# One transformer layer in fp32: 40 projection panels as quarter products, both branch projections behind them

## The reference, cut to what matters

```python
h = rmsnorm(x, norm_mix_g)                      # x: 512 tokens x 2048, float32
q_a, k_a, v_a, q_b, k_b, v_b = split(h @ w_in)  # widths 1024, 256, 256, 1024, 1024, 1024
o_a = swa_sink_attention(rope(q_a), rope(k_a), v_a, sinks)
o_b = stick_breaking_attention(q_b, k_b, v_b)
y_a, y_b = o_a @ w_branch_a, o_b @ w_branch_b   # 1024 -> 2048
gates = sigmoid(h @ w_gate + b_gate).reshape(S, 2, 2048)
x = x + (gates[:, 0] * y_a + gates[:, 1] * y_b) @ w_out
x = x + memory_cross_attention(rmsnorm(x), rmsnorm(mem), ...)
x = x + swiglu(rmsnorm(x), w_gu, w_down)        # hidden width 5632
return rmsnorm(x)
```

## Time and profile before

| | |
|---|---|
| median of three runs | 2746.04 us |
| the profiled execution: span, first to last instruction (what lies around it has no record of its own) | 2743.1 us |
| TensorE busy | 2704.5 us |
| VectorE busy | 1737.1 us |
| ScalarE busy | 1017.7 us |
| GpSimd busy | 766.3 us |
| HBM read and written | 301.27 and 30.41 MB |

### The profile page before, as it was taken

One profiled execution on the slowest core, in us unless ns is written; L12 is line 12 of the kernel. 1 busy time (PEld: TensorE's weight loads), 2 busy tenths in 40 slices (PEclk: granted clock), 3 DMA queues, 4 the chain that ended last, 5 costly groups with the idle time before them and its releaser, 6 DMA issues.

```text
span 2743.1 us, 34950 instructions
## 1 busy us (share of the span) xinstructions
PE 2704.5 (99%) x13710; PEld 2279.2 (83%) x13710; DVE 1737.1 (63%) x1820; ACT 1017.7 (37%) x1134; POOL 766.3 (28%) x642
## 2 busy tenths in 40 slices
PE   9999999999999999999999999999999999999997
PEld 7888888888778888888788888888888888888886
DVE  6677652334653344573677767687777777777786
ACT  6555432224642232243553333333333332222224
POOL 0000000000000003330357666776667632212120
PEclk9999999999999999999999999999999999999999
DMA  6221233322222325333434444434343463444432
GB/s 239 77 85 62 83 97 99 92 84 92 77 93 92 99 77 207 93 121 109 139 109 137 132 138 132 138 101 146 127 143 127 143 238 123 161 146 137 161 125 82
DMA packets 125889, 333.29 MB, mean 121 GB/s; under 512 B 10320, under 2 KB 57424, under 8 KB 125136
## 3 DMA queue, kind: packets, MB, share of 16 engines
q1 hardware_dynamic: 119296, 309.37, 35.3%
q10 hardware_dynamic: 6480, 22.35, 2.0%
HBM read 301.27 MB, written 30.41 MB: 121 GB/s over the span
## 4 chain that ended last, share of the span: by engine, by line
PE 92%; DVE 4%; ACT 1%; DMA 1%; issue 1%; SPq 0%; DVEq 0%; ACTq 0%
PE ps L2198 16%; PE acc L1812 14%; PE acc L1814 14%; PE acc L1813 14%; PE ps L2201 8%; PE acc L1832 6%; PE acc L1834 6%; PE acc L1833 6%; PE acc L2198 3%; PE acc L2201 1%; DMA x_tokens<-x_n 1%; PE ps L1874 1%; PE ps L1863 1%; DVE w_lo L1588 1%; ACT ps L799 0%
## 5 line engine op out<-in xcount | busy, mean ns | idle before, releaser
L1101 DVE TENSOR_TENSOR w_lo<-raw,w_hi 128x1024 fp32r<-128x1024 f32 x328 | 475.9, 1456 | 274.9 <-ACT w_hi L609 274.3
L1812 PE MATMUL acc<-act_both,w_hi 128*128 128x512 f32 (+1 forms) x1536 | 591.1, 385 | 3.6 <-DVE w_lo L1101 3.1
L1814 PE MATMUL acc<-act_both,w_lo 128*128 128x512 f32 (+1 forms) x1536 | 585.3, 381 | 0.0
L1813 PE MATMUL acc<-act_both,w_hi 128*128 128x512 f32 (+1 forms) x1536 | 584.9, 381 | 0.0
L609 ACT ACTIVATE w_hi<-raw 128x1024 fp32r<-128x1024 f32 x328 | 344.3, 1055 | 553.9 <-PE acc L1814 340.7
L1812 PEld LDWEIGHTS acc<-act_both,w_hi 128*128 128x128 f32 x1536 | 289.6, 189 | 59.4 <-DVE w_lo L1101 3.7
L1814 PEld LDWEIGHTS acc<-act_both,w_lo 128*128 128x128 f32 x1536 | 289.5, 188 | 55.4
L1813 PEld LDWEIGHTS acc<-act_both,w_hi 128*128 128x128 f32 x1536 | 289.8, 189 | 54.3 <-issue 0.7
L543 POOL MEMSET mem_stat<- 128x256 f32 x1 | 0.3, 312 | 1047.1 <-DMA mem<-mem_t 1047.1
L2198 PE MATMUL ps<-t_both,w_hi 128*128 128x512 f32 x896 | 281.6, 396 | 0.5 <-DVE cg L1616 0.5
L1832 PE MATMUL acc<-act_both,w_hi 128*128 128x512 f32 x672 | 262.9, 391 | 3.1 <-DVE x L1456 3.0
(11 more groups left out here) (306 smaller groups left out, 4752.8 us busy)
## 6 DMA issues: line engine op xcount, KB each, us to landing
raw<-w_stream SPq DMA_DIRECT2D x412, 512.0 KB, 3.6
over<-w_stream SPq DMA_DIRECT2D x84, 512.0 KB, 4.4
gate_t<-cg ACTq DMA_DIRECT2D x22, 512.0 KB, 2.6
over<-gate_t SPq DMA_DIRECT2D x22, 512.0 KB, 5.3
up_t<-cu ACTq DMA_DIRECT2D x20, 512.0 KB, 2.6
over<-up_t SPq DMA_DIRECT2D x20, 512.0 KB, 6.2
x<-x_t SPq DMA_DIRECT2D x16, 512.0 KB, 8.6
x_tokens<-x_n SPq DMA_DIRECT2D x4, 1024.0 KB, 15.4
```

The source lines that it names most:

```text
L1101: nc.vector.tensor_tensor(w_lo[:, s, :], raw[:, s, :], f(w_hi[:, s, :]), ALU.subtract)\
L1812: nc.tensor.matmul(dst, wh, ah, start=start and k == 0, stop=False)
L1813: nc.tensor.matmul(dst, wh, al, start=False, stop=False)
L1814: last = nc.tensor.matmul(dst, wl, ah, start=False, stop=stop and k == UK - 1)
```

## The change

The order of the weight stream and of all engines' programs from 365 us on is new:

- Only v0, v1, k0 and q0 stay direct panels (8 units, `U_V`); the first four of these units are multiplied inside `sb_last`, where gate units were.
- k1, q1 to q7 and all 32 gate panels become 20 pairs of quarter products (`U_H`, 80 mix units). For this GpSimd scales `x` by the norm's gain and makes its sums during stick-breaking, ScalarE and VectorE split them (`mixed_high`, `mixed_low`), and every pair goes out to HBM (`h_t`) and comes back later.
- The stick-breaking result goes out raw (`ob_t`) instead of being split on chip; it is read back and split at the end of the quarter products (`ob_high`, `ob_low`).
- The 16 units of branch projection B (`U_BB`) are the fillers of local attention, now one unit each (`FILLERS` 3, 3, 3, 2 with 3 ahead and 2 behind). ScalarE copies each product to `merged` (`branch_copy`).
- The 16 units of branch projection A (`U_BA`) follow. For each pair of outputs VectorE scales four gate tiles by the norm (L1690, 128 x 2048), ScalarE takes four sigmoids, and VectorE multiplies and adds.

In all, 120 direct units between stick-breaking's last pass and the output projection (the four inside it included) become 40 direct units and 80 mix units.

```diff
+U_V = U_SB + PAIRS * 6
+U_H = U_V + 4 * 2
+H_PAIRS = 4 + 2 * KT // 2
+H_UNITS = 4 * H_PAIRS
+U_BB = U_H + H_UNITS
+U_BA = U_BB + KT
+U_OUT = U_BA + KT
-FILLERS = (4, 6, 3, 3)
+FILL_FIRST, FILL_LAST = 3, 2
+FILLERS = (3, 3, 3, 2)
...
             def o_high(par_):
-                nc.scalar.activation(o_hi[rows, pair.at(), :], ps[par_][rows, 0:S], ACT.Copy)\
-                    .then_inc(o_hi_done, 1)
+                nc.scalar.activation(zb[par_][rows, 0:S], ps[par_][rows, 0:S], ACT.Copy).then_inc(ps_free, 1)
+                act.wait_ge(ps_free, hd.at(3 + par_))
+                act.dma_start(ob_t[pair.at(), rows, :], zb[par_][rows, 0:S]).then_inc(ob_stored[par_], 16)
...
+            mixed_low(0, 0)
+            while converted.n < U_H:
+                units()
+            mixed_low(1, 0)
+            mix_low(5)
+            for p in range(H_LOOPS):
+                dve.wait_ge(pair_stored[1], 16 * p) if p else None
+                read_products(2 * p, cg)
+                mix_low(2)
...
+                if p < H_LOOPS - 1:
+                    mix_low(2)
+                else:
+                    mix_low()
+                    ob_low(0)
+                    units()
+                    ob_low(1)
+                dve.wait_ge(pair_stored[0], 16 * (p + 1))
+                read_products(2 * p + 1, cu)
+                if p < H_LOOPS - 1:
+                    mix_low(4)
...
             for d in range(DUOS):
                 swa_max(d, 0)
                 swa_max(d, 1)
                 swa_prob(d, 0)
+                units()
                 swa_prob(d, 1)
                 if d < DUOS - 1:
                     rope(ROTATED[d][0])
-                    units(2)
+                    units()
                     rope(ROTATED[d][1])
...
+            for j in range(KT // 2):
+                part = gates_of(j)
+                dve.wait_ge(gates_in[j % 4], 32 * (j // 4 + 1))
+                nc.vector.tensor_tensor(part, part, rstd[:].unsqueeze(1).unsqueeze(1).broadcast_to([P, 2, 2, S]),
+                                        ALU.mult).then_inc(gates_scaled, 1)
+                for b in range(2):
+                    m = 2 * j + b
+                    if converted.n < U_OUT + AHEAD:
+                        units()
+                    ga, gb, dst = part[:, 0, b, :], part[:, 1, b, :], merged[:, m, :]
+                    dve.wait_ge(acc_free, A_BB + m + 1)
+                    dve.wait_ge(sig_ready, 4 * j + 2 * b + 1)
+                    link(nc.vector.tensor_tensor(dst, dst, gb, ALU.mult))
+                    dve.wait_ge(sig_ready, 4 * j + 2 * b + 2)
+                    unit.add()
+                    dve.wait_ge(unit_done, unit.at())
+                    nc.vector.tensor_tensor(ga, output()[:], ga, ALU.mult).then_inc(acc_free, 1)
+                    dve.wait_ge(acc_free, out_no.at())
+                    nc.vector.tensor_tensor(dst, dst, ga, ALU.add).then_inc(mix_ready, 1)
+                if j > 1:
+                    merged_low(2 * j - 4, 2)
+            while converted.n < U_OUT + AHEAD:
+                units()
+            merged_low(KT - 4, 4)
...
+            for d in range(DUOS):
+
+                swa_scores(d, 0)
+                swa_scores(d, 1)
+                filler()
+                swa_turn(d, 0)
+                filler()
+                swa_values(d, 0)
+                swa_turn(d, 1)
+                filler(FILLERS[d] - 2)
+                swa_values(d, 1)
+            filler(FILL_LAST)
+            for m in range(KT):
+                unit(output()[:], [oa_tile(k) for k in range(UK)], True, True,
```

More of the change, by code:

```diff
@@ L240, in block_kernel @@
         with ExitStack() as a:
+            sb("place_of_products", [P, 22 * UK * P // 4], F32, a)
             cos_t = sb("cos_t", [P, S], F32, a)
             sin_t = sb("sin_t", [P, S], F32, a)
+        with ExitStack() as a:
+            gate_pairs = [sb(f"gate_pair{n}", [P, 2, 2, S], F32, a) for n in range(2)]
+        with ExitStack() as a:
             ka = sb("ka", [P, S], F32, a)
@@ new lines, in mix_sums @@
+            def mix_sums(first, end):
+                for n in range(first, end):
+                    part = mix_raw(n)
+                    pool.wait_ge(mix_in[n % 4], 16 * (n // 4 + 1))
+                    link(nc.gpsimd.tensor_tensor(part[:, 4, :], part[:, 0, :], part[:, 1, :], ALU.subtract))
+                    link(nc.gpsimd.tensor_tensor(part[:, 5:7, :], part[:, 0:5:4, :],
+                                                 part[:, 3:4, :].broadcast_to([P, 2, 2 * P]), ALU.add))
+                    nc.gpsimd.tensor_tensor(part[:, 7, :], part[:, 2, :], part[:, 6, :], ALU.subtract)\
+                        .then_inc(sums_made, 1)
@@ L851, in merged_high @@
                     nc.scalar.activation(act_hi[:, m, :], merged[:, m, :], ACT.Copy).then_inc(mg_hi, 1)
-            gates(gate_a, B_GATE, merged_high)
+            for j in range(KT // 2):
+                act.wait_ge(gates_scaled, j + 1)
+                for b in range(2):
+                    for a, first in ((1, KT), (0, 0)):
+                        sigmoid(gates_of(j)[:, a, b, :], B_GATE + first + 2 * j + b)
+                    units()
+                if j > 1:
+                    merged_high(2 * j - 4, 2)
+            while converted.n < U_OUT + AHEAD:
+                units()
+            act.wait_ge(unit_done, U_OUT)
+            merged_high(KT - 4, 4)
+            out_no.n = A_OUT
             with repeat(act, KT // 4, [(converted, 4)]):
@@ new lines, in _ @@
+            mixed_low(0, 0)
+            while converted.n < U_H:
+                units()
+            mixed_low(1, 0)
+            unit.n = U_BB
+            out_no.n = A_BB
+            mix_low(5)
+            for p in range(H_LOOPS):
+                dve.wait_ge(pair_stored[1], 16 * p) if p else None
+                read_products(2 * p, cg)
+                mix_low(2)
+                if p == 0:
+                    angles()
+                if p == 1:
+                    two_angles()
+                if p == 2:
+                    scaled_angles()
+                if p < H_LOOPS - 1:
[3 more added lines that the diff above has]
+                    ob_low(0)
+                    units()
+                    ob_low(1)
+                dve.wait_ge(pair_stored[0], 16 * (p + 1))
+                read_products(2 * p + 1, cu)
+                if p < H_LOOPS - 1:
+                    mix_low(4)
@@ L1417, in _ @@
                 tr.add()
-            units(2)
-            rope(1)
-            units(2)
+            units()
             rope(2)
-            units(2)
+            units()
             for d in range(DUOS):
@@ new lines, in mix_groups @@
+            def mix_groups(first, end, outputs):
+                for g in range(first, end):
+                    if g - first < 2:
+                        pe.wait_ge(acc_free, outputs - 1 + g - first)
+                    for c in range(4):
+                        if g == 0 and c in (0, 2):
+                            pe.wait_ge(t_lo_done, 4 + 2 * c)
+                        mix_unit(g, c)
+            panel(act_tile)
+            panel(act_tile)
+            assert u.n == U_H and out_no.n == A_BB
@@ L2038, in _ @@
                 tr.add()
-            for _ in range(3):
-                panel(act_tile)
+            filler()
             pe.wait_ge(va_ready, 2)
-            fill = Tally()
-            def filler():
-                if fill.n % 2 == 0:
-                    fill_dst.append(output()[:])
-                unit(fill_dst[-1], second if fill.n % 2 else first, fill.n % 2 == 0, fill.n % 2 == 1)
-                fill.add()
-            fill_dst = []
             for d in range(DUOS):
@@ L2306 @@
 HEADS = [h + o * GQ for h in LOWER for o in (0, 1)]
-def gates_and_branches(w_gate, w_branch):
-    gates, branches = ([stream(columns(w, m)) for m in range(KT)] for w in (w_gate, w_branch))
-    parts = gates[:2]
-    for m in range(0, KT, 2):
-        parts += branches[m:m + 2] + gates[m + 2:m + 4]
-    return parts
 def weight_stream(w_in, w_gate, w_a, w_b, w_out, w_xq, w_xkv, w_xo, w_gu, w_down):
```

661 lines of the change are left out of this document (362 added, 299 removed).

## The result

The change makes the kernel slower: 2855.68 us median (2854.62 to 2857.44) against 2746.24, a ratio of 1.0401 with a 95% interval of 1.0386 to 1.0415. The forecast was 2813 with a range up to 2845: the sign was right, the size too small by 43 us.

The account below looks back on a forecast made before the run. TensorE was taken to bound the kernel. Terms -43.4, +1, +1, +9, +11.5, +71.4 and +17 gave +67.5 us on the profiled 2743.1, so 2810.6; with 2.9 for the median, 2813 us, range 2786 to 2845.

Parts of the forecast that it names:

- Branch A: Branch projection A: each unit's low part on VectorE waits for the unit before, so TensorE stalls between units; +71.4 us (65 to 80).
- Groups to branch B: From the last quarter-product group to the first attention scores: TensorE waits for copies, a low part and rotations; +9 us (5 to 12).
- local attention: Block seams without filler, block 1's third rotation and block 3 without filler make TensorE wait; +11.5 us (6 to 16).
- E+12.0: Time counted from E, the end of the last quarter-product group; the second branch unit's low part was expected 12.0 us later.
- Stick-breaking: GpSimd's work on `x` slows VectorE beside it, but the passes have fillers; +1 us (0 to 5).
- The clock: TensorE's granted clock falls after stalls, costing 1.5 to 1.7 us behind longer ones, half behind others; +17 us (0 to 35).
- the two more: Two further clock falls, in front of branch A, counted in the clock's +17 us.
- Start of the groups: First quarter-product group: short lead as activations are prepared, +1 us (0 to 3); rotation angles cost nothing, up to 4 without cover.
- The term for the work removed: Twenty pairs move from direct panels to quarter-product groups on TensorE, saving 2.17 us each: -43.4 us.
- the third rival: VectorE's chain in branch A does not hold TensorE, so only the other terms count: 2725 us, chance 0.05.

## Why the forecast was too low

- **Branch A**, the deciding term, was right: +71.4 forecast, 67.9 measured, and taking the cause away brought back 95 us, waits and clock together. The chain was the one described, down to 2.84, 5.04 and 6.24 for 3.05, 5.2 and 6.45, each 0.2 too long.
- **Groups to branch B** (+9, was 8.9) and **local attention** (+11.5, was 8.4 and 4.0 of clock) had the right waits at the right places. That the sums come so near is in part luck: both terms are idle time, 20.5 us together, of which 15.0 came, and longer matmuls made up for the rest. (The second branch unit's low part, put at E+12.0, is at E+12.5 by the forecast's own rows; the unit started at E+11.5.)
- **Stick-breaking** was the first step that failed: "The passes have fillers, so I take +1 (0 to 5)". The forecast counted GpSimd's 45 us of work and had a row of a slow low part, but spread the slowdown over passes with room. All of it fell into the first pass, where nothing had been made ahead and nearly every instruction on VectorE's chain with two SBUF operands took 0.7 to 1.1 us longer. It cost 19.4, 12.1 of waits and 7.3 of clock behind them; the same work begun behind the scans and spread over four passes costs nothing.
- **The clock** was the second: "I take the full 1.5 to 1.7 for the longer ones, half for the others". The sum is too low by its own words: eight in full and eight by half at 1.5 to 1.7 are 18.0 to 20.4 us before the two more, where the term is 17. And the halves were wrong: all eight short waits brought the clock down. The price was 1.84 us behind a short wait (0.12 of it stays when the clock does not fall) and 2.32 behind a long one. Behind a short wait the clock came back after some 3.4 us, as in the earlier trace rows; in a long one it fell before the unit began and stayed at 0.50 longer, from 990 to 996 us in the windows shown. So 15 units paid, 31.0 us. The Trainium skill (TensorE: Matmul & The Clock Gate, HAM oscillation — how this bites in real kernels) describes bursts of matmuls that are shorter than the wait behind them, of which every single one starts cold; here the units, 5.44 us of work, were longer than most of the waits, and all were slowed. The fall also showed behind branch A (2.7), in local attention (4.0), and where the forecast had no clock at all, in stick-breaking and in the groups.
- **Start of the groups** was the third: "VectorE has a quarter of 19.6 us free", so the angles were to cost nothing. They cost a wait of 4.0 us, since in the first groups there is no lead to draw on. The bound named there ("up to 4 us") was right for the wait, and 1.7 us of clock came behind it; the other waits of the groups were left out. Moving the angles gave little, so a part of the 9.4 stays without a shown cause.
- The term for the work removed, -43.4, was right at the steady group's price. With the two large losses undone the kernel is at 2742, not at the 2725 of the third rival. That rival has 22.5 us for the start, the groups, the way to branch B and local attention; these take 30.7. Some 5 more stay in branch A even with a lead, and the last 4 were not placed.

## What to carry to other kernels

When a loop loses an instruction that stood between two others, look at what is left in order behind the wait: a conversion that was three units ahead can fall to none, and then two engines take turns. A single unit of lead was enough here, but for five waits of 0.8 us. And ask of any work given to GpSimd which operands it reads, and whether the chain beside it on VectorE reads two from SBUF at a moment without a lead; starting it behind that chain and spreading it over four passes was worth 19 us.

## What the runs showed of the hardware

- With both engines reading SBUF, VectorE's low parts and scans, two operands from SBUF each, took 1.75 times (2134 against 1220 ns) and 2.1 times (1672 against 804 ns) as long on average, and the loss was 0.7 to 1.1 us for one instruction nearly whatever its length. Those with an operand in PSUM took as long as before, and GpSimd's own sums of 512 columns up to 2.4 us in place of 1.29. Beside GpSimd instructions that only write, low parts and scans showed no difference; four scalings of 128 x 128 took 1.39 us together in place of 0.88.
- The length of a wait alone did not decide whether TensorE's clock fell. A wait of 2.84 us brought it from 1.00 to 0.50 in every one of eight cases in branch A, but that of 2.82 us ahead of 1359.18 in the same execution did not, as the window behind it shows, nor did that of 2.16 us in the kernel before; one of 2.29 us ahead of 2367.69 did. Filling the waits with useless matmuls was worth 26 us.

```profile
1359.18:1365.00 5.82, 5.82 (x48) 5.82 (x49) 5.79 (x8) 2.59 (x3) 0.00 (x0) 1.00 0.64 194
```
